# Rotating the queries and keys of the second block: TensorE's permutation matmul or VectorE's shuffle

## The reference, cut to what matters

```python
u = jnp.einsum('btd,de->bte', rmsnorm(x, norm1_g[l]), w_in[l])
(mq, mk, mv, mo, mi, mf, aq, ak, av, hq, hf, hi, hg) = jnp.split(u, ...)
# diff_attention(aq, ak, av, ...): 4 heads x 2 halves of 64
q = rmsnorm(q, qn_g); k = rmsnorm(k, kn_g)        # over each 64
q = partial_rope(q, pos); k = partial_rope(k, pos) # first 16 of each 64
#   r1 = x1 * cos - x2 * sin;  r2 = x2 * cos + x1 * sin   (x1, x2: 8 each)
q = q * 64 ** -0.5
```

## Time and profile before

| what | value |
|---|---|
| median of three runs | 3468.72 us (3467.31 to 3468.8) |
| the profiled execution, its own time | 3470.07 us |
| its span in the trace | 3468.3 us |
| PE busy | 3410.0 us, 98% |
| DVE, ACT, POOL busy | 40%, 29%, 44% |
| granted TensorE clock, mean | 0.994 of full speed |

### The profile page before, as it was taken

How to read it: one execution, slowest core, us unless ns; L and a number is a source line. 1 busy time by engine, 2 the same in 40 slices (tenths; PEclk the granted TensorE clock), 3 DMA queues, 4 the chain that set the end, 5 groups by cost and what they waited for, 6 DMA issues and landing times.

```text
span 3468.3 us, 41846 instructions
## 1 busy us (share of the span) xinstructions
PE 3410.0 (98%) x16720; PEld 2748.6 (79%) x16720; DVE 1393.4 (40%) x2596; ACT 1012.3 (29%) x1275; POOL 1510.3 (44%) x522
## 2 busy tenths in 40 slices
PE   8999999899999999999999999999999999999999
PEld 7878878588888888886888887877888878778887
DVE  6565248735253524136312126854101158541010
ACT  2222322622223212224322233443212234442121
POOL 3545552035455545540354564502645545025453
PEclk9999999999999999999999999999999999999999
DMA  7444222024353443212222222201222212012222
GB/s 281 181 155 182 102 85 74 1 104 188 139 191 119 183 150 142 95 49 69 73 86 102 90 99 73 74 25 49 97 97 97 97 68 79 25 49 97 96 96 75
DMA packets 58748, 358.65 MB, mean 103 GB/s; under 512 B 10208, under 2 KB 10592, under 8 KB 21856
## 3 DMA queue, kind: packets, MB, share of 16 engines
q1 hardware_dynamic: 58592, 356.50, 28.6%
HBM read 354.38 MB, written 2.10 MB: 103 GB/s over the span
## 4 chain that ended last, share of the span: by engine, by line
PE 94%; DVE 3%; ACT 1%; issue 1%; DMA 1%; SPq 0%; POOL 0%; DVEq 0%; ACTq 0%
PE LP L572 85%; PE XB L572 8%; ACT E L1351 1%; DMA big<-w_ada 1%; PE LP L950 0%; PE XB L795 0%; DVE XB L2068 0%; PE XB L831 0%; ACT sq L1351 0%; DVE big L2248 0%; DVE big L2250 0%; DVE S L2424 0%; DVE big L2247 0%; DVE u L2909 0%; DVE h L2315 0%
## 5 line engine op out<-in xcount | busy, mean ns | idle before, releaser
L1855 POOL TENSOR_TENSOR w_lo<-ring,w_hi 128x2048 fp32r<-128x2048 f32 (+3 forms) x275 | 1134.4, 4125 | 700.0 <-ACT w_hi L1351 699.8
L572 PE MATMUL LP<-u_hi,w_hi 128*128 128x512 f32 x2448 | 959.5, 392 | 2.6 <-ACT u_hi L1351 2.4
L572 PE MATMUL LP<-u_hi,w_lo 128*128 128x512 f32 x2448 | 954.4, 390 | 0.0
L572 PE MATMUL LP<-u_lo,w_hi 128*128 128x512 f32 x2448 | 934.9, 391 | 0.0
L572 PE MATMUL LP<-big_r,w_hi 128*128 128x512 f32 x2520 | 780.3, 390 | 4.9 <-DVE h L2315 2.5
L1351 ACT ACTIVATE w_hi<-ring 128x2048 fp32r<-128x2048 f32 (+3 forms) x275 | 474.4, 1725 | 749.7 <-PE LP L572 746.8
L572 PE MATMUL LP<-big_r,w_lo 128*128 128x512 f32 x1508 | 587.5, 390 | 0.0
L572 PEld LDWEIGHTS LP<-big_r,w_hi 128*128 128x128 f32 x2520 | 472.6, 188 | 106.1 <-DVE h L2315 4.2
L572 PEld LDWEIGHTS LP<-u_hi,w_hi 128*128 128x128 f32 x2448 | 460.5, 188 | 111.6 <-issue 16.1
L572 PEld LDWEIGHTS LP<-u_lo,w_hi 128*128 128x128 f32 x2448 | 462.4, 189 | 96.2 <-issue 0.5
L572 PEld LDWEIGHTS LP<-u_hi,w_lo 128*128 128x128 f32 x2448 | 460.5, 188 | 95.8
(11 more groups left out here) (353 smaller groups left out, 3497.6 us busy)
## 6 DMA issues: line engine op xcount, KB each, us to landing
ada_in<-w_ada SPq DMA_DIRECT2D x66, 1024.0 KB, 4.9
ring<-w_in SPq DMA_DIRECT2D x20, 1024.0 KB, 4.8
ring<-w_gu00a SPq DMA_DIRECT2D x11, 1024.0 KB, 7.1
ring<-w_gu00b SPq DMA_DIRECT2D x11, 1024.0 KB, 6.6
ring<-w_gu01a SPq DMA_DIRECT2D x11, 1024.0 KB, 6.6
ring<-w_gu01b SPq DMA_DIRECT2D x11, 1024.0 KB, 6.7
ring<-w_gu10a SPq DMA_DIRECT2D x11, 1024.0 KB, 6.6
ring<-w_gu10b SPq DMA_DIRECT2D x11, 1024.0 KB, 4.9
```

The source lines that it names most:

```text
L572: return pe.matmul(o, lhsT=lhsT, rhs=rhs, start=start, stop=stop)
L1855: gp.tensor_tensor(w_lo[:, slab % RING, 0:width], ring[:, slab % RING, 0:width], w_high(q, width).bitcast(F32), ALU.subtract).then_inc(s(" ...
```

## The change

The second network's q and k no longer go through `rotate`. ScalarE takes each q and k slab out of PSUM, times the gains, behind its squares, and frees the PSUM tile. GpSimd's `cosines` waits for that instead of a matmul. VectorE swaps the eights by a shuffle inside 32 partitions into XB[1] or XB[2], multiplies by the sines (whose sign is now folded into the table), waits for the cosines and adds. The wait of the third pair of sums moves from `qk_root` to `qk_recip`. Four small operations join the chain of constants. The turns of the first network stay as they are.

```diff
--- before.py
+++ after.py
@@ -370,6 +370,13 @@
             return XB[3 * (n % 2)][:, 0:(n // IDX_H + 2) * P]
 
         masks = wk[:, 4, 0:2 * P]
+
+        def key_gain(l):
+
+            return st[:, 12 + l:13 + l]
+
+        turn_sign = st[:, 14:15]
+        TURNED = [8, 9, 10, 11, 12, 13, 14, 15, 0, 1, 2, 3, 4, 5, 6, 7] + list(range(16, 32))
 
         def select_tile(qb):
 
@@ -1076,7 +1083,7 @@
 
                     pe.wait_ge(s("qk_squared"), 4 * l + pair + 1)
                     if pair == 2:
-                        pe.wait_ge(s("qk_root"), 2 * l + 1)
+                        pe.wait_ge(s("qk_recip"), 2 * l + 1)
                     for i in range(2):
                         c = 2 * (pair % 2) + i
                         last = mm(XB[0][0:40, :], half_sums(c, 40), big[:, 22 + c, :], start=c == 0, stop=c == 3)
@@ -1117,10 +1124,8 @@
                     if k == 5:
                         qk_spread(1)
                     if k == 2:
-                        pe.wait_ge(s("gates_scaled"), 2 * (l + 1))
+                        pe.wait_ge(s("gates_scaled"), 2 * l + 1)
                     if 2 <= k < 6:
-                        slab_taken(k - 1)
-                        rotate((AQ + 2 * k - 4, AQ + 2 * k - 3), cc("rot16"))
                         qk_sums(k - 2)
                     if k == 6:
                         qk_spread(3)
@@ -1704,6 +1709,10 @@
                         act.wait_ge(s("lin_done"), pl.slab + k)
                         c = 22 + 2 * ((k - 1) % 2)
                         f(big[:, c:c + 2, :], LP[(first + k) % 2][:, :, :], ACT.Square).then_inc(s("qk_squared"), 1)
+                        c = AQ + 2 * k - 2
+                        gains = sp_("qn", l) if k < 3 else key_gain(l)
+                        f(big[:, c:c + 2, :], LP[(first + k) % 2][:, :, :], ACT.Copy, scale=gains)\
+                            .then_inc(s(f"lin_taken{(first + k) % 2}"), 1)
                     if k == 1:
                         f(gate_rest(0), XB[2][64:68, :], ACT.Copy)
                         f(gate_rest(1), XB[2][96:100, :], ACT.Copy).then_inc(s("gates_moved"), 1)
@@ -2025,9 +2034,22 @@
                     gp.tensor_tensor(z[:, :, 1, :], z[:, :, 1, :], q[:, :, 1, :], ALU.mult)\
                         .then_inc(s("z_ready"), 1)
 
+                first = pl.group - 1
+
+                def cosines(k):
+
+                    g = first + k
+                    gp.wait_ge(s(f"lin_taken{g % 2}"), g // 2 + 1)
+                    for i in range(2):
+                        r = pl.rope + i
+                        gp.wait_ge(s("rope_done"), r - 1)
+                        gp.tensor_tensor(Z[:, r % 2, :], big[:, AQ + 2 * k - 2 + i, :], cc("diff_cos"), ALU.mult)\
+                            .then_inc(s("rope_cos"), 1)
+                    pl.rope += 2
+
                 def behind_slab(k):
                     if 1 <= k < 5:
-                        turn((AQ + 2 * k - 2, AQ + 2 * k - 1), cc("diff_cos"), Z)
+                        cosines(k)
                     if k >= 6:
                         level_inputs(k - 5)
 
@@ -2273,6 +2295,10 @@
                 link(ts(gate_w[:, :, 0:64], gate_flat, 1.0, None, ALU.mult))
                 link(tt(gate_w[:, :, 64:128], gate_flat, gate_w[:, :, 0:64].bitcast(F32), ALU.subtract))
                 ts(gate_w[:, :, 128:GATE_W], gate_flat[:, :, 0:GATE_W - P], 0.0, None, ALU.mult).then_inc(s("gate_cols"), 1)
+                link(dve.tensor_reduce(turn_sign, cc("rot16"), AX.X, ALU.add))
+                link(ts(cc("diff_sin"), cc("diff_sin"), turn_sign, -1.0, ALU.mult, ALU.mult))
+                for l in range(DEPTH):
+                    link(ts(key_gain(l), sp_("kn", l), -0.125, None, ALU.mult))
                 lb = sp_("lb", 0, 4)
                 link(tt(st[:, 16:18], lb[:, 0:2], lb[:, 2:4], ALU.max))
                 for l in range(DEPTH):
@@ -2703,7 +2729,18 @@
                     dve.nop().then_inc(s("gates_rows"), 1)
 
                 def turn_qk(k):
-                    turn((AQ + 2 * k - 2, AQ + 2 * k - 1), cc("diff_sin"), Z[:, 0:2, :])
+
+                    g = pl.group - 1 + k
+                    dve.wait_ge(s(f"lin_taken{g % 2}"), g // 2 + 1)
+                    for i in range(2):
+                        c, r = AQ + 2 * k - 2 + i, pl.rope + i
+                        sines = XB[1 + r % 2][:, :]
+                        link(dve.stream_shuffle(sines, big[:, c, :], TURNED))
+                        link(tt(sines, cc("diff_sin"), sines, ALU.mult))
+                        dve.wait_ge(s("rope_cos"), r + 1)
+                        tt(big[:, c, :], sines, Z[:, r % 2, :], ALU.add).then_inc(s("rope_done"), 1)
+                    pl.rope += 2
+                    dve.wait_ge(s("rope_done"), pl.rope)
 
                 def qk_recip(i):
 
@@ -2785,12 +2822,7 @@
                 def in_taken(k, it, p):
                     c = 2 * IN_ORDER[k]
                     k += 1
-                    if 1 <= k < 5:
-                        pl.got("qk_squared")
-                        gains, sign = (sp_("qn", l), 1.0) if k < 3 else (sp_("kn", l), -0.125)
-                        ts(big[:, c:c + 2, :], LP[p][:, :, :], gains, sign, ALU.mult, ALU.mult)\
-                            .then_inc(s(f"lin_taken{p}"), 1)
-                    else:
+                    if k >= 5:
                         tt(big[:, c:c + 2, :], LP[p][:, :, :], over_two(R), ALU.mult).then_inc(s(f"lin_taken{p}"), 1)
                     def scale_stream(chunks):
                         for i in chunks if l == 0 else ():
```

## The result

The changed kernel takes 3475.68 us (median of 11 runs, 3474.01 to 3478.7). The kernel before took 3468.8 us (11 runs, 3467.31 to 3471.29) beside it. The ratio is 1.0019, with a 95% interval of 1.0011 to 1.0027: about 6.9 us slower where I had forecast 4.6 us faster. It lies outside the range of 3457 to 3469. The profiled execution took 3475.86 us with a span of 3474.1, 5.8 us longer than the span before.

What follows compares the result with a forecast made beforehand. TensorE, 94% of the chain that ended last, was taken to bound the kernel. Two layers gaining 5.8 us, less 1.2 for the constants, made 4.6 us: 3468.72 - 4.6 = 3464.1 us, range 3457 to 3469.

Steps and rivals of the forecast that it cites:

- The removed work: Second network's rotations leave TensorE: 32 records gone, 7.46 us a layer, 14.9 us for two layers if TensorE never waits.
- The new instructions: VectorE's shuffle of 128x512 taken as 0.73 us, ScalarE's copy of a slab out of PSUM as 1.0 us.
- The slower case, a dear shuffle: Rival: the shuffle takes up to 3.35 us, behind the cosines at each wait; 3477.3 us at that bound, chance 0.07.
- The first and the second wait: New TensorE waits per layer: third pair of sums, middle of slab 4, and spread, middle of slab 6; 2.2 us each.
- The constants: Four operations added to the constants' chain lengthen TensorE's 2.46 us wait for weights one to one, by 1.2 us.
- "Per layer: 7.46 - 2.2 - 2.2 = 3.06 us gained": Each layer gains the rotations' time less two new waits; 6.1 us for both layers, 5.8 after semaphore reactions.
- "It is hidden with 0.7 us to spare. Behind that, VectorE is paced by TensorE as before": No third late place: VectorE's `tokw` copy, before the recurrence's first level, comes 19.0 us after `qk_scale(2)`; TensorE needs 19.7.
- a wait in slab 7 would prove me wrong: Sign against the forecast: a TensorE wait in slabs 7 to 10 or at the maps' start that wasn't there before.

Runs made afterwards that it cites:

- the last experiment: The same run as Experiment 12: 3456.09 us, ratio 0.9966 to the kernel before.
- Experiment 1: The kernel before with only the four added constant operations in VectorE's chain: 3472.93 us, ratio 1.0008.
- Experiment 9: The changed kernel with the negated running maximum moved behind the `tokw` copy: 3474.77 us, ratio 1.0014 to the kernel before.
- Experiment 12: As 8, with `qk_scale(2)` before taking slab 5, GpSimd's sixth subtraction waiting for the gates, and TensorE's scales and the `tokw` copy before the running sums: 3456.09 us.
- 10: The changed kernel with the negation moved, the constants made later, and the waits in slabs 4 and 6 filled with four dummy matmuls each: 3465.86 us.
- 4: The changed kernel with dummy matmuls ahead of the waits in slabs 4 and 6, and in slab 7 of the second layer: 3480.11 us.
- 6: The changed kernel with both chunks' shuffles and sine products ahead of both additions, before the first wait for the cosines: 3477.67 us.
- 7: The changed kernel with GpSimd's cosines of a q or k slab ahead of its weight subtraction: 3473.68 us.
- 8: The changed kernel with shuffles ahead of the cosine wait, cosines ahead of the subtraction, and the four constant operations in later VectorE idle time: 3469.15 us.
- 11: As 8, with the negated maximum deferred and `qk_scale(2)` ahead of the taking of slab 5: 3471.61 us.

## Why the prediction was wrong

**The removed work: right.** The 32 records are gone and with them the 7.46 us a layer; the last experiment gets 13.1 of the 14.9 back. One small term was missed: the first matmul of a pair of sums, which a rotation used to cover, starts more slowly behind the products of a slab, some 0.4 us a layer.

**The new instructions: right.** Shuffle 0.69 us (0.73 taken), copy 1.11 (1.0 taken). The slower case, a dear shuffle, is ruled out; that the measured time falls among that rival's times is chance.

**The first and the second wait: right in place, releaser and length.** 2.10, 2.18, 2.08, 2.19 us for 2.2 each.

**The constants: right as a wait, wrong as a price.** The wait is 3.67 for 2.46 + 1.2. That these "come on top of this wait, one to one" is where it fails: behind the longer wait the clock was low in all eight profiles that have it, worth 1.7 us more. Experiment 1 measured 3.3 us of loss for 1.2 of chain, with 0 to 5.9 in its interval.

**"Per layer: 7.46 - 2.2 - 2.2 = 3.06 us gained" is the step that failed first.** It prices a wait at its length. The kernel before had no idle time in these slabs and the clock stood at 1.00; I read this as a fact of the stage, and gave no term to a change of it. That the clock can fall behind a wait of this length stood in the trace of before, behind the 2.51 us at 2288. The low clock took 1.7 us behind the constants, 2.8 to 3.1 behind the first layer's second wait and 3.55 behind the third wait, some 8.3 us in the profiled execution. The Trainium skill (TensorE: Matmul & The Clock Gate, "What's actually happening") says that 1.2 GHz is the level of an idle TensorE and that work brings it back to 2.4. The traces agree behind the waits (0.50 and 0.57, and 1.00 again some matmuls later), and add that one wait of 2.2 us among hundreds of busy matmuls can be followed by it. In the trace of before it also fell at 2080 with TensorE busy for 4.00 of the 4 us from 2077.

**"It is hidden with 0.7 us to spare. Behind that, VectorE is paced by TensorE as before" is the other step that failed.** I only compared the `tokw` copy with TensorE's pace. I did not ask what the loss of `qk_scale(2)`'s lead of 1.23 us does to an instruction 7.5 us later that GpSimd can hold. The rows to see it were in the trace of before: a margin of 0.73 us, and a scan at 3.52 us that usually takes 1.22. The third wait costs 2.75 us, and more by the clock behind it. That a wait in slab 7 would prove me wrong stood in the prediction; it did.

**The sum of it**, by TensorE's marks after less before: the constants +2.85, less 1.33 by which the execution was ahead in the first network; the first layer +0.4 (-7.46, sums 0.4, waits 2.1 and 2.2, clock 3.1); the second +3.7 (-7.46, sums 0.4, waits 2.1, 2.2 and 2.75, clock 3.55). Together 5.6 of the 5.8. Told by causes against the forecast gain of 4.6: less 0.7 for the sums, less 2.75 for the third wait, less 6.9 for the low clock in the whole trace, which makes 5.75 lost.

**How far this is shown.** The third wait comes from the held instruction. Experiment 9 moves the negation alone, and both are gone. Over all 14 profiles, each with two layers, the negation or the addition before it was held in 14 layers; 13 of them have the wait in slab 7, the other one has it filled, and of the 14 layers without a hold none has it. Experiment 12 fits this, but changes more than the order. That the low clock makes the rest is shown by the clock records (6.9 us) and by the two layers of experiment 9, and 10 agrees. That the waits bring the falls is argued from how often they follow:

| wait of TensorE | places in the profiles | clock low behind it |
|---|---|---|
| 0.93 to 1.31 us, slabs 4 and 6 | 8 | 0 |
| 2.08 to 2.22 us, slabs 4 and 6 | 16 | 5 |
| 2.44 to 2.47 us, constants | 6 | 2 |
| 2.51 us, later in the first layer, in all kernels | 14 | 12 |
| 3.65 to 3.81 us, constants | 8 | 8 |
| 2.73 to 3.95 us, slab 7 | 13 | 13 |

The two causes hide each other: where the clock is low in slab 6 the subtraction comes later and nothing is held, and where the wait is filled the hold is back (4). Open is what decides, behind a wait of 2.1 to 2.5 us, whether the clock falls.

## What to carry to other kernels

Where TensorE has no idle time at all, taking work from it makes it wait, and such a wait may cost more than its length: price it at its length plus, here, up to 3.6 us of half clock, and look for work to reorder, or for filler, before you take the work away. Before you change the lead of one engine over another, list the instructions that VectorE runs near a long GpSimd instruction and that show several lengths for one form, with their margins: which of the two starts first decided over 4 us here, and a shift of 1.1 us turned it. Ordering the pair with a semaphore, together with the reorderings of 6, 7, 8 and 11, turned a change that lost 7 us into one that gains 13. The semaphore isn't an idle one: it is what released the subtraction in both layers, and TensorE still didn't wait for the weights.

## What the runs showed of the hardware

- TensorE's granted clock went to its lower level behind 40 of the 65 waits in the table above: never behind 0.93 to 1.31 us, sometimes behind 2.08 to 2.51, always behind 2.73 to 3.95. One fall cost 1.7 to 3.6 us. It also fell with no wait ahead of it, behind 32 matmuls of 128x1 (0.58 over 2080 to 2084 in the kernel before).
- Some VectorE instructions on SBUF alone that start while GpSimd subtracts end 0.03 to 1.1 us after it does: 0.42 to 4.58 us (one input, 4x512), 0.68 to 4.85 and 0.68 to 4.88 (two inputs, 4x512), 1.22 to 3.52 (scan, 128x512), 0.17 to 2.65 (one input, 128x8, beside a subtraction of 128x1408). Instructions with one input in PSUM ran beside it at their usual 1.22 and 1.27, and so did MAX8 and MATCH_REPLACE8 on SBUF alone, at 0.69 and 0.68.
- The shuffle inside 32 partitions of 128x512, from SBUF to PSUM, takes 0.69 us, as the two-operand instructions do; the load of its list shows 0.01.
